# Seven products for three value projections in each of two layers, and one set of weight sums moved ahead of the conditioning work

## What is computed

```
h = rms_norm(x, norm2_w[i])
g, u = jnp.split(h @ w_up[i], [D_FF], axis=-1)        # D_FF = 2816
g = depthwise_conv_centered(g, ffn_conv_w[i], ffn_conv_b[i])   # 3 taps
x = x + (jax.nn.silu(g) * u) @ w_down[i]
```

## Time and profile before

| | |
|---|---|
| median of three runs | 2420.58 us (2420.38 to 2421.92) |
| the profiled execution | 2421.49 us, of which the span is 2419.8 us |
| TensorE busy | 2393.0 us, 99% |
| VectorE busy | 1595.8 us, 66% |
| VectorE busy in the up projections of the first stack, 242.20 to 376.24 us and 682.20 to 817.50 us | 111.03 of 134.04 us, and 124.85 of 135.30 us |
| granted TensorE clock | 0.999 of full speed |
| DMA in those two stretches | 318 and 335 GB/s |

### The profile page before, as it was taken

The page is one execution under the profiler, slowest core; times in us unless marked ns, Lnnn a source line. Parts: engine busy times, 40 slices in busy tenths (PEclk is TensorE's granted clock), DMA queues, the critical chain, the costliest instruction groups (busy, mean ns, idle before and its releaser), DMA issues.

```text
span 2419.8 us, 41521 instructions
## 1 busy us (share of the span) xinstructions
PE 2393.0 (99%) x17196; PEld 2179.9 (90%) x17196; DVE 1595.8 (66%) x3331; ACT 705.0 (29%) x1436; POOL 154.6 (6%) x268
## 2 busy tenths in 40 slices
PE   9999999999999999999999999999999999999998
PEld 7879999987899898999998899898889999889998
DVE  6653887566289837698744489954456985327983
ACT  3441110144311121533032233213423331443321
POOL 2000100000021000011000032011000000000000
PEclk9999999999999999999999999999999999999999
DMA  7935985574399646589454398743334555335552
GB/s 218 239 93 180 338 305 186 148 189 115 105 343 311 235 154 183 198 310 308 146 176 134 110 343 309 235 149 123 105 122 143 171 165 166 123 105 169 163 166 96
DMA packets 403270, 458.36 MB, mean 189 GB/s; under 512 B 50751, under 2 KB 374776, under 8 KB 403084
## 3 DMA queue, kind: packets, MB, share of 16 engines
q1 hardware_dynamic: 370098, 340.53, 45.0%
q0 software_dynamic: 29936, 112.73, 12.8%
q10 hardware_dynamic: 3050, 2.46, 0.4%
HBM read 451.48 MB, written 1.29 MB: 187 GB/s over the span
## 4 chain that ended last, share of the span: by engine, by line
PE 88%; DVE 8%; issue 1%; DMA 1%; ACT 1%; POOL 0%; DVEq 0%; SPq 0%; ACTq 0%; POOLq 0%
PE job_bank L995 35%; PE job_bank L1071 26%; PE job_bank L1050 11%; PE mix_bank L1050 4%; PE job_bank L1540 4%; DVE sb_arena L2909 2%; DVE sb_arena L2953 1%; PE mix_bank L1487 1%; PE job_bank L1515 1%; PE mix_bank L1459 1%; DVE sb_arena L3018 1%; PE mix_bank L1501 1%; PE mix_bank L1026 0%; PE mix_bank L1831 0%; PE job_bank L1263 0%
## 5 line engine op out<-in xcount | busy, mean ns | idle before, releaser
L995 PE MATMUL job_bank<-sb_h,sb_ring 128*128 128x256 f32 x3616 | 807.1, 380 | 0.8 <-DVE sb_h L3189 0.8
L995 PEld LDWEIGHTS job_bank<-sb_h,sb_ring 128*128 128x128 f32 x3616 | 674.5, 189 | 99.4 <-issue 9.2
L2909 DVE SCALAR_TENSOR_TENSOR sb_arena<-sb_arena,sb_c_act 128x512 f32<-128x512 f32 x336 | 252.8, 752 | 11.0 <-DVE sb_arena L2909 0.5
L3018 DVE SCALAR_TENSOR_TENSOR sb_arena<-sb_arena,sb_par 128x256 f32<-128x256 f32 x440 | 204.3, 506 | 9.2 <-ACT sb_arena L2072 5.3
L1050 PE MATMUL job_bank<-sb_h,sb_ring 128*128 128x128 f32 x1600 | 184.1, 275 | 1.4 <-ACT sb_h L2375 1.4
L1050 PEld LDWEIGHTS job_bank<-sb_h,sb_ring 128*128 128x128 f32 x1600 | 181.2, 192 | 1.8 <-issue 1.6
L1071 PE MATMUL job_bank<-sb_t,sb_ring 128*128 128x128 f32 x1248 | 165.5, 275 | 0.0
L2072 ACT ACTIVATE sb_arena<-sb_arena,sb_par 128x256 f32<-128x256 f32 x220 | 120.2, 593 | 135.8 <-DVE sb_arena L2985 125.5
L1071 PE MATMUL job_bank<-sb_h,sb_ring 128*128 128x128 f32 x1152 | 152.8, 276 | 0.0
L1071 PEld LDWEIGHTS job_bank<-sb_t,sb_ring 128*128 128x128 f32 x1248 | 152.2, 192 | 0.0
L1071 PEld LDWEIGHTS job_bank<-sb_h,sb_ring 128*128 128x128 f32 x1152 | 144.3, 192 | 6.1 <-issue 3.3
(11 more groups left out here) (515 smaller groups left out, 3172.7 us busy)
## 6 DMA issues: line engine op xcount, KB each, us to landing
sb_arena<-in_ada_w POOLq DMA_DIRECT2D x96, 1024.0 KB, 7.6
sb_ring<-in_ffn_w_up SPq DMA_DIRECT2D x88, 1024.0 KB, 5.2
sb_ring<-in_w_up SPq DMA_DIRECT2D x44, 1024.0 KB, 6.5
sb_ring<-in_ffn_w_down SPq DMA_DIRECT2D x32, 1024.0 KB, 5.2
sb_ring<-in_w_in SPq DMA_DIRECT2D x24, 1024.0 KB, 6.4
sb_ring<-in_w_down SPq DMA_DIRECT2D x16, 1024.0 KB, 5.8
sb_ring<-in_hg_w_in SPq DMA_DIRECT2D x16, 1024.0 KB, 5.5
sb_ring<-in_ml_w_up SPq DMA_DIRECT2D x16, 1024.0 KB, 5.5
```

The costliest lines, as they stand in the source:

```text
L995: mm = pe.matmul(o, st, mv, start=(k0 + k == 0 and t == 0), stop=(k0 + k == kn - 1), skip_group_check=True)
L2909: ins = vec.scalar_tensor_tensor(out=o, in0=w, scalar=col, in1=o, op0=ALU.mult, op1=ALU.add)
L3018: ins = vec.scalar_tensor_tensor(out=o, in0=fraw[:, i % 2, v, j:j + T], scalar=pcol(column, (l * FFN_TAPS + j) * width + c), in1=o, op0=AL ...
```

## The change

- In each of the two layers of the first stack the values u3, u6 and u9 become fast jobs. They have a copy space of their own (`value_kept`). VectorE makes their forms after the taps of the pair before, and their join, with the product after it, is done at the head of the next pair (`join_value`), behind the first conditioning half of that pair.
- The forms of the first unit of d2 are made directly behind those of d1, ahead of the addition of d0 and the two conditioning halves. That is done in all four blocks that carry conditioning. The form slot that they use lies elsewhere, outside the two ring slots that the last conditioning pieces occupy.
- The corner is copied twice side by side (256 elements in place of 128), so that a join is one VectorE instruction of 512 elements in place of two of 256. The joins of the down projection change alike. This holds for all fast jobs.

```diff
+FIRST_VALUES = (3, 6, 9)
...
-                      in_row(ada_at + 11 * quarter_n)]
+                      three_quarters(ada_at + 6 * quarter_n, ada_at + 7 * quarter_n) + quarters_of(h_flat, 4)[3:]]
...
-            return gates[1:] if stack == 1 else [gates[i] for i in FAST_PAIRS]
+            if stack == 1:
+                return [job for i in range(1, FT // 2) for job in (gates[i], values[i])[:2 if i in FIRST_VALUES else 1]]
+            return [gates[i] for i in FAST_PAIRS]
...
-                act.activation(parts_of[fast_no[job[0]]][:, 3 * P:4 * P], L[job[0] % 4][:, 3 * P:4 * P], ACT.Copy)\
+                corner = L[job[0] % 4][:, 3 * P:4 * P].unsqueeze(1).to_broadcast([P, 2, P])
+                act.activation(parts_of[fast_no[job[0]]][:, 3 * P:5 * P].rearrange("p (t n) -> p t n", t=2), corner, ACT.Copy)\
...
                         keep_mid(g)
+                        if values[i - 1][0] in fast_no:
+                            keep_corner(values[i - 1])
                         gate(i - 1)
+                        if u[0] in fast_no:
+                            keep_mid(u)
                         keep_corner(g)
...
-            def join_tiles(job, first, second):
+            def join_tiles(job, dst):
-                upper, lower, bank = add_mid(job)
-                vec.tensor_tensor(first, bank[:, 0:T], upper, ALU.add).then_inc(s.raw_joined, 1)
-                vec.tensor_tensor(second, bank[:, T:2 * T], lower, ALU.add).then_inc(bank_read[job[0] % 4], 1)
-                own(s.raw_joined, due(s.raw_joined))
+                sums, bank = add_mid(job)
+                vec.tensor_tensor(dst, bank, sums, ALU.add).then_inc(bank_read[job[0] % 4], 1)
...
+                def join_value(i, u):
+                    made = fact[:, 2 * i:2 * i + 2, :]
+                    join_tiles(u, made)
+                    vec.wait_ge(s.sg_ready, due(s.sg_ready))
+                    read_out(vec, u)
+                    vec.tensor_tensor(made, made, fcv[:, i % 2, 0:2, :], ALU.mult).then_inc(s.act_ready, 1)
...
                 for i, (g, u) in enumerate(zip(gates, values)):
-                    if i < FT // 2 - 1 and gates[i + 1][0] in fast_no:
+                    held = i and values[i - 1][0] in fast_no
+                    fast_value = u[0] in fast_no
+                    if held:
+                        ada_half()
+                        join_value(i - 1, values[i - 1])
+                    if i < FT // 2 - 1 and gates[i + 1][0] in fast_no and not fast_value:
                         more_forms(1)
                     if g[0] in fast_no:
-                        join_tiles(g, *(fraw[:, i % 2, v, off:off + T] for v in range(2)))
-                    ada_half()
+                        join_tiles(g, fraw[:, i % 2, 0:2, off:off + T])
+                    if fast_value:
+                        more_forms(1)
+                    if not held:
+                        ada_half()
                     read_out(vec, g)
                     other_taps(stack, l, i, 0)
+                    if i < FT // 2 - 1 and values[i + 1][0] in fast_no:
+                        more_forms(1)
                     ada_half()
+                    if fast_value:
+                        continue
...
                 row_forms(fact[:, 16:FT, :], cond_fform[2])
-                more_forms(1)
+                more_forms(2)
...
-                    more_forms((3, 0)[i - 1])
+                    more_forms((2, 0)[i - 1])
```

62 lines of the change are left out of this document (33 added, 29 removed).

## The result

| | before | changed |
|---|---|---|
| median of 11 runs | 2421.92 us (2420.38 to 2422.96) | 2427.10 us (2426.17 to 2432.39) |
| ratio | | 1.0029 (1.002 to 1.0037) |
| profiled execution, its span | 2421.49, 2419.8 us | 2426.17, 2424.4 us |

The change costs 5.2 us in the medians and 4.7 in the profiled executions. Its runs are spread over 6.2 us, those of the kernel before over 2.6, and its profiled execution is the fastest of its eleven.

The account below looks back on a forecast made before the run. The prediction took TensorE's own work plus its waits to bound the kernel. Its terms, -3.9 - 6.2 + 6.4 + 7.7 = +4.0 us, gave a median of 2424.6 us, with an 8-in-10 range of 2417 to 2429 us.

Parts of the forecast that it names:

- (a) to (c): Waits: 1 us at g4, g7, g10, both layers; at u3 (3.6 us), u6, second layer only; none at d2's first products.
- (d): Pairs from g3 to d0 take longer than before: 1.2 us in the first layer, 9 us in the second.
- Seven products: Six values become fast jobs on TensorE, 6.25 us each against 6.91 plain: 3.9 us saved.
- Moved forms: At d2's first products in four blocks, earlier forms remove TensorE's waits: 6.2 us saved.
- Waits behind the joins: At g4, g7, g10 of both layers, forms stand behind the previous gate's join: 6 x 1.06 = 6.4 us lost.
- First layer, the rest: Forms of u3, g5, u6, u9 arrive in time, with half a microsecond's cover at each value: costed at nothing.
- Second layer: GpSimd's tap weights delay VectorE: 3.6 us at u3, 1.7 at g4, 2.4 at u6, 7.7 us beyond the join waits.
- The clock: Outside the sum, only a rival: granted clock falls to 1.2 GHz behind second-layer waits, 6.3 us more.
- rival 3: Granted clock falls to 1.2 GHz between 712 and 726 us in the second layer: 6.3 us more, 2430.9 us; chance 0.07.
- Rival 1: Second layer's late work lands elsewhere; u3, g4 or u6 wait less; without any of 7.7 us, 2416.9 us; chance 0.27.
- Rival 2: TensorE finds its forms in time and keeps the whole gain: -10.1 us, 2410.5 us; chance 0.06.
- rival 4: Second layer's lateness is carried on through g8 and u9: 2 to 5 us more, 2427 to 2430 us; chance 0.12.

Follow-up runs that it names:

- all three moves: Changed kernel with next gate's forms ahead of the join, first four conditioning loads ahead of tap loads, GpSimd's tap instructions behind the last conditioning load: 2417.84 us, ratio 0.9986.

## Why the prediction was right, and where its terms were off

The forecast was +4.0 us in the profile; it came to +4.7, and 2427.1 us in the median lies within the range, above the forecast's own band of 2422.5 to 2426.7. The signs (a) to (c) of the prediction came as written; of (d), the first layer grew by 1.55 us (forecast 1.2) and the second by 10.92 (forecast 9). By its terms:

- **Seven products, -3.9.** A fast job takes 6.25 us as before; the pairs fit with 6 x 0.66. Not measured apart.
- **Moved forms, -6.2.** The stretch from d0 to d2's first products became 0.87, 1.23, 2.04 and 2.05 us shorter in the four blocks, and the half alone gave 6.6 us. Nothing was late for it. Shown.
- **Waits behind the joins, +6.4.** Mechanism and place as forecast: 1.07 us at each, and 0.10 more since the row that waited takes 1.16 us and not 1.06. The step mis-sized is that I left this tenth out: 6 x 1.17 = 7.0. Moving the forms ahead of the join took the waits away in the first layer, so the order is the cause; gaps of 0.23 us at the three gates and 0.36 at u6 and u9 remained there, 1.4 us in all, which keeps three fast values there at 0.6 us gained, not 2.0.
- **First layer, the rest, 0.** Right: its stretch grew by 1.55 us, and 3 x 1.17 - 1.98 is 1.53.
- **Second layer, +7.7.** It came to 4.34 at u3 (forecast 3.6), 2.59 at u6 (2.4), none beyond 1.17 at g4 (1.7), the wait at g5 back at its old size: 6.9 us. At g4 GpSimd's instruction fell on the addition of the copied quarters (the row at 721.45, 2.73 us for 0.28), while TensorE was busy; it stretched nothing on the way, and no run shows whether a join, with one input in PSUM, would have passed beside it. That VectorE's lateness makes these waits is shown by the run with all three moves, in which they went. What I had named as its cause was only half of it: the other half is a load. GpSimd issues the four conditioning loads behind the tap loads, and VectorE waits 2.3 to 8.8 us for the first, 1.9 us of the wait at u3. The row was in the trace of before and not in my walk, which began at 711.23.
- **The clock, not in the sum, +2.4.** This is the step that failed in kind: rival 3, to which I gave 0.07, came true on top of the forecast. I argued that waits of 1 to 2 us had left TensorE's pace alone, which was true, and set that against a forecast of 3.6 us at u3, for which no row spoke. Its price was less than the 6.3 us I gave it, since I had all seven rows of F and L at half pace, and the clock was back at 1.00 from 722 us on: 2.4 us for three rows of block products. The Trainium skill (TensorE: Matmul & The Clock Gate, Why this matters for your kernels), whose warning I had cited and priced at a small chance, is borne out by the windows above.
- **Not in the sum at all, -1.6.** The profiled execution of the change began its first fast gate 0.3 us earlier and had no wait at 553.69 us (0.72 us there before, behind VectorE, which had got its row data 2.6 us later), 0.8 us by the starts of the rows; some 0.3 us more lie between the second and the third d0, the rest in pieces of 0.1. I take these for differences from one execution to the next, which no run tests.

-4.0 - 6.2 + 7.0 + 6.9 + 2.4 - 1.6 = +4.5 us, against +4.6 in the span. Without the last term it is +6.1; the medians differ by 5.2. So forecast and result agree closely in part by luck: 1.7 us forecast at g4 that didn't come, and 1.6 us that no term had, stand against a clock that I had left out.

Rival 1 (the late work lands elsewhere) was right at g4 alone, where its mechanism took 1.7 us off, and wrong as a whole, since u3 waited more than forecast. Rival 2 (the whole gain) was wrong; even with all three moves 1.4 us of each layer's 2.0 stay in small gaps. The median lies in the range of rival 4 (2427 to 2430 us), but not by its mechanism: behind u6 no wait is longer than the 0.91 us behind a join, and none is at u9.

No version with fast values beats the moved forms alone (2414.7 us, ratio 0.9969). That half is what is worth keeping as it is.

## What to carry to other kernels

Before a set of operations is added to the engine that is second busiest, walk it from its last true idle moment, not from the row where the new work begins: here the debt at u3 was made of a load 30 us earlier and of two instructions of another engine that stretched its own. An order written by hand can move a wait between consumers without making it smaller; it shrinks only when the debt does. And price a wait of several microseconds on TensorE with the clock behind it, 1.6 to 2.6 us more in the rows of these runs.
